# Eight expert rounds on one core: the two weight splits beside the last turned product are held back, and the output leaves in four transfers

## The reference

```python
def moe_swiglu(h, w_router, w_gate, w_up, w_down):
    ...
    logits = (xf @ w_router).astype(jnp.float32)
    top_logits, top_idx = lax.top_k(logits, TOP_K)      # TOP_K = 2
    gates = jax.nn.softmax(top_logits, axis=-1)
    ...                                                 # rows sorted by expert, in blocks of 128
    def expert_block(args):
        tok, e = args
        xb = xf[tok]
        hb = jax.nn.silu(xb @ w_gate[e]) * (xb @ w_up[e])
        return hb @ w_down[e]
    ...                                                 # weighted by the gates and added per token
```

## Time and profile before

| | us |
|---|---|
| median of 3 runs | 2028.63 |
| the three runs | 2028.44, 2028.63, 2031.82 |
| span of the profiled execution (first to last instruction) | 2030.7 |
| the only one of the three times that is longer than that span | 2031.82 |
| TensorE busy in the span | 1940.3 (96%) |
| VectorE busy | 1566.0 (77%) |
| ScalarE busy | 1241.0 (61%) |
| chain that ended last, TensorE's share | 84% |
| the eight rounds, from the first gate product to the last sum | about 985 |

### The profile page before, as it was taken

One profiled execution on the slowest core, in us unless ns is written; L12 is line 12 of the kernel. 1 busy time (PEld: TensorE's weight loads), 2 busy tenths in 40 slices (PEclk: granted clock), 3 DMA queues, 4 the chain that ended last, 5 costly groups with the idle time before them and its releaser, 6 DMA issues.

```text
span 2030.7 us, 26201 instructions
## 1 busy us (share of the span) xinstructions
PE 1940.3 (96%) x9320; PEld 1619.0 (80%) x9320; DVE 1566.0 (77%) x1881; ACT 1241.0 (61%) x1461; POOL 160.4 (8%) x228
## 2 busy tenths in 40 slices
PE   8989988899989899999999999999999999999998
PEld 6867877778778788888878878888888888888886
DVE  7765966867656654446878898989889898998987
ACT  5562145645654544344767767777777777777775
POOL 4113401313011000000000000000000000000000
PEclk9999999999989999999999999999999999999999
DMA  8422234324324255553459999899999989999994
GB/s 330 157 84 104 93 125 140 125 104 180 113 82 178 92 207 187 187 187 125 187 229 382 355 353 376 343 382 351 372 375 349 376 342 385 353 373 374 341 376 174
DMA packets 71802, 504.78 MB, mean 249 GB/s; under 512 B 8864, under 2 KB 8864, under 8 KB 11808
## 3 DMA queue, kind: packets, MB, share of 16 engines
q1 hardware_dynamic: 70432, 498.87, 64.8%
q0 software_dynamic: 1280, 4.72, 0.6%
HBM read 501.46 MB, written 2.10 MB: 248 GB/s over the span
## 4 chain that ended last, share of the span: by engine, by line
PE 84%; DVE 8%; ACT 5%; issue 2%; POOL 1%; DMA 0%; DVEq 0%; SPq 0%; ACTq 0%; POOLq 0%
PE psum L1022 24%; PE psum L1024 24%; PE psum L1023 24%; PE psum L1958 4%; DVE low L989 3%; ACT high L986 2%; PE psum L3486 1%; PE psum L1966 1%; ACT h L1694 1%; PE psum L3417 0%; PE psum L1974 0%; DVE small L1738 0%; PE psum L1566 0%; DMA const<-in_constants 0%; PE psum L1143 0%
## 5 line engine op out<-in xcount | busy, mean ns | idle before, releaser
L989 DVE TENSOR_TENSOR low<-raw,high 128x2048 fp32r<-128x2048 f32 x459 | 1044.9, 2281 | 265.5 <-ACT high L986 261.9
L986 ACT ACTIVATE high<-raw 128x2048 fp32r<-128x2048 f32 x459 | 876.9, 1912 | 371.3 <-PE psum L1024 352.6
L1022 PE MATMUL psum<-high,yT_high 128*128 128x512 f32 (+1 forms) x1672 | 664.6, 397 | 25.9 <-DVE yT_low L3695 6.5
L1024 PE MATMUL psum<-high,yT_low 128*128 128x512 f32 (+1 forms) x1672 | 653.3, 391 | 0.0
L1023 PE MATMUL psum<-low,yT_high 128*128 128x512 f32 (+1 forms) x1672 | 652.1, 390 | 0.0
L1022 PEld LDWEIGHTS psum<-high,yT_high 128*128 128x128 f32 x1672 | 315.5, 189 | 95.6 <-issue 14.2
L1024 PEld LDWEIGHTS psum<-high,yT_low 128*128 128x128 f32 x1672 | 315.3, 189 | 67.1
L1023 PEld LDWEIGHTS psum<-low,yT_high 128*128 128x128 f32 x1672 | 316.0, 189 | 61.0
L1022 PE MATMUL psum<-high,hT_high 128*128 128x512 f32 (+2 forms) x560 | 220.8, 394 | 1.6 <-DVE low L1006 0.9
L1024 PE MATMUL psum<-high,hT_low 128*128 128x512 f32 (+2 forms) x560 | 217.3, 388 | 0.0
L1023 PE MATMUL psum<-low,hT_high 128*128 128x512 f32 (+2 forms) x560 | 217.3, 388 | 0.0
(11 more groups left out here) (367 smaller groups left out, 1714.9 us busy)
## 6 DMA issues: line engine op xcount, KB each, us to landing
raw<-in_moe_weights SPq DMA_DIRECT2D x336, 1024.0 KB, 4.9
raw<-in_weights SPq DMA_DIRECT2D x132, 1024.0 KB, 4.9
raw<-in_weights SPq DMA_DIRECT2D x2, 896.0 KB, 4.7
raw<-in_weights SPq DMA_DIRECT2D x2, 768.0 KB, 8.1
x<-in_x SPq DMA_DIRECT2D x2, 512.0 KB, 3.9
raw<-in_weights SPq DMA_DIRECT2D x2, 512.0 KB, 3.6
rows<-h POOLq DMA_DIRECT2D x1, 1024.0 KB, 4.8
out_x<-x SPq DMA_DIRECT2D x1, 1024.0 KB, 5.5
```

Source lines behind the costliest of these rows:

```text
L986: eng.activation(high, raw, ACT.Copy).then_inc(k.high_ready, 1)
L989: eng.tensor_tensor(low, raw, high.bitcast(F32), ALU.subtract).then_inc(k.low_ready, 1)
L1022: pe.matmul(out, lhs.high, rhs.high, start=start, stop=False)
L1024: return pe.matmul(out, lhs.low, rhs.high, start=False, stop=stop)
```

## The change

Two things are changed. The steps that begin no split are now "down first 5" and turn 6, on ScalarE and on VectorE alike. And the store waits for each of the four scatter parts by itself and issues a transfer of 256 KB for it, before it waits for all four.

```diff
+HELD = (("down first", FF_STEPS - 2), ("turn", FF_STEPS - 1))
...
-def moe_wait_all(k, sp):
-
-    k.wait_released(sp, ("moe", "scatter", 3), (k.more + (N_EXPERTS - 1)) * 2)
+def moe_wait_scatter(k, sp, i):
+
+    k.wait_released(sp, ("moe", "scatter", i), (k.more + (N_EXPERTS - 1)) * 2)
...
-            if (kind, i) != ("turn", FF_STEPS - 1):
+            if (kind, i) not in HELD:
                 done = split_round(k, act, done, index, t)
...
-            if (kind, i) != ("turn", FF_STEPS - 1):
+            if (kind, i) not in HELD:
                 done = split_round(k, v, done, index, t)
...
+    rows = k.out[0].rearrange("(t p) d -> p t d", p=P)
     if layers[-1] == "moe":
-        moe_wait_all(k, sp)
-    else:
-        for name in out_names(layers[-1]):
-            k.wait_released(sp, name)
-    sp.dma_start(k.out[0].rearrange("(t p) d -> p t d", p=P), k.x[:, :, :]).then_inc(k.stored, 16)
+        for i in range(4):
+            moe_wait_scatter(k, sp, i)
+            half, tile = i // 2, i % 2
+            cols = slice(512 * half, 512 * (half + 1))
+            sp.dma_start(rows[:, tile, cols], k.x[:, tile, cols]).then_inc(k.stored, 16)
+        sp.wait_ge(k.stored, 64)
+        return
```

## The result

| | before | changed |
|---|---|---|
| median, us (5 runs each) | 2028.63 | 2037.83 |
| lowest and highest, us | 2025.77, 2031.82 | 2035.51, 2040.69 |
| ratio to before, 95% interval | | 1.0051 (1.0039 to 1.0062) |
| span of the profiled execution, us | 2030.7 | 2038.9 |

The change makes the kernel slower, by 9.2 us in the medians. The forecast was 2035.5, and 2037.83 lies in its range. In the experiments further down, one run of e3_hold_last (2195.32) and one of e4_short_gather (2203.34) were slow executions, with a mean granted clock of 0.85 and 0.84 instead of 0.99, and the ratios leave them out.

What follows compares the result with a forecast made beforehand. TensorE was taken as the bound, busy 84% of the span. Held splits cost 8.9 us and the store saves 2.0, so 6.9 more on the 2028.63 median gives 2035.5; range 2031.5 to 2039.5.

Steps and rivals of the forecast that it cites:

- Direction and mechanism: At each round's tail the turn's wait goes, but held splits delay down 6 and gate 0; 6.9 us slower in all.
- The common round: Rounds 1 to 6: gate 0 starts 1.2 us later, including 0.28 from down 6's later start.
- I give it no chance of its own: Rival that the clock falls behind a longer wait; dismissed because it was 1.00 around round 0's 2.2 us wait.
- Sum of the held splits: Loss over the rounds: 6 x 1.2 + 1.7 = 8.9 us, with round 7 losing nothing.
- upper bound of the forecast: Held splits' loss if VectorE's whole lag reached TensorE each time: 7 x 1.65 = 11.6 us.
- The wait behind round 0: TensorE's wait for granule 3, after VectorE's list of overfull experts: near 2.7 us instead of 2.2.
- The store: At the kernel's end, four 256 KB transfers instead of one of 1 MB: 2.0 us saved.
- a sign: At the kernel's end, the last of four stores should land 3 to 3.5 us after its issue.
- From span to time: Whole kernel: time about 1.1 us over span if the 2031.82 run was profiled; the difference was added to the median.
- ScalarE isn't the limit there: Before gate 0, ScalarE has the next round's high 0 at about 1895.1, ahead of VectorE's low from 1895.95.
- The loads: Loads into raw places freed some 3.4 and 3.1 us later at a round's tail: costed at nothing.
- The rival of the removed wait: Before down 6 the wait is simply removed: 7 x 0.95 + 2.0 = 8.7 us less, 2019.9; chance 0.05.

Runs made afterwards that it cites:

- e3_hold_last: The changed kernel, but only granule 41's split held until behind turn 6, granule 40 begun as before the change; 2025.53 us, ratio to before 0.9984.
- e4_short_gather: The changed kernel with six of eight pieces of the gathered tokens' low left out on VectorE in rounds 0 to 7; 2029.07 us, ratio to before 1.0009.
- e1: The changed kernel with the output leaving in one transfer as before, so only the two splits held; 2041.46 us, ratio to before 1.0052.
- e2: The changed kernel with the order of splits of before, so only the store in four transfers; 2025.35 us, ratio to before 0.9984.
- e5: The changed kernel with VectorE's list of overfull experts cut into five pieces beside gates 1 to 5 of round 0; 2032.29 us, ratio to before 1.0022.
- e8: The changed kernel with only granule 41 held and the next round's granule 0 split ahead of the gathered tokens; 2019.22 us, ratio to before 0.9955.
- e9: The changed kernel, both splits held, with the next round's granule 0 split ahead of the gathered tokens; 2033.31 us, ratio to before 1.0027.

## Why the prediction was right, and where it was short

- **Direction and mechanism were right.** Down 6 later by 0.23 in round 6 (1900.52 - 1898.30 = 2.22 behind the gather against 1.99; forecast 0.28), gate 0 later by 1.12 (forecast 1.2). The wait for the turn goes (6.5 us in seven waits, none after). Down 6 waits for low 40 instead, 1.18 where 1.24 was expected. Gate 0 waits behind VectorE's longer queue. e1 and e2 show that the hold is the whole loss.
- **The common round was 0.2 short** (1.39 against 1.2). Gate 0's distance from the gather grew by 1.12 in round 6 and by 8.88 - 7.54 = 1.34 in round 2 (1412.21 - 1403.33 after, 1407.95 - 1400.41 before). I took 0.08 between the end of a low and TensorE's start. In round 2 it is 0.24 (low 0 ends at 1411.97, the matmul starts at 1412.21), and the first matmul behind a wait holds its follower off by 0.34 instead of 0.23. The changed kernel has two waits a round where before had one, so it pays this once more.
- **"I give it no chance of its own" was wrong of the clock.** The step took round 0's 2.2 us wait with a clock of 1.00 as proof that a wait of this size is free. Behind a wait of 2.31 it was not: 1.6 us, which makes 3.24 of the expected 1.7 (VectorE's delay itself cost 1.63, as forecast). In e5, where the wait is gone, the clock stays at 1.00. What else it takes isn't known: the changed kernel had waits of 1.29 and 0.85 ahead of the 2.31, but e4 had 1.29 ahead of 2.33 and kept its clock, and e8 lost it with none ahead of 2.85.
- **Sum of the held splits:** forecast 8.9, trace 11.6; 1.6 of the gap of 2.7 is the clock, the rest the 0.2 in each of six rounds. That 11.6 is also the upper bound of the forecast (7 x 1.65) is a coincidence: VectorE's lag didn't reach TensorE in full each time.
- **The wait behind round 0** was to be near 2.7 and is 2.31. TensorE came to it 1.54 later than before (1.63 - 0.09), not 1.2, so that more of VectorE's 1.63 was already spent.
- **The store** was forecast at 2.0 and brought 1.8. The fixed 2.75 and 0.7 of data were nearly right: 3.45 against a longest landing of 3.7, just outside the 3 to 3.5 that were named as a sign, and 5.5 - 3.7 is the 1.8. The median landing of the four is 2.3, but the end counts the last one.
- **From span to time:** the profiled run was taken for the one at 2031.82, 1.1 over its span. In the changed kernel and in all runs of the experiments the time is 1.8 to 1.9 over the span, so it was none of the three. Nothing hangs on it, because the difference was added to the median.
- **"ScalarE isn't the limit there" held** for the changed kernel: high 0 ends at about 1903.8, 0.9 ahead of low 0's start at 1904.66. e4 shows it as the next limit.
- **The loads** were hidden, as costed: from 1150 us on, ScalarE's table of waits names no transfer in the changed kernel.
- **The rival of the removed wait** gave 0.95 a round as its price. e3 shows that even a turn and a low 40 in time would have brought only 0.3, since gate 0's own chain had only 0.6 to spare. Taken alone that rival was overpriced three times; with that chain moved ahead as well (e8) it was worth 1.18.

## What to carry to other kernels

A wait names the last thing that was late, not what it would bring to remove it: before an order is changed, measure how far ahead of its need each of the next two or three items is, since the smallest of these is all that can be won. When two engines work off a queue for a third, work held back for an urgent item is paid by everything behind it; hold back no more than the item needs (here one split of two), and then order the rest by when it is needed. A wait that is inherited from another cause (here a list of small instructions behind round 0) takes every delay in full, and is worth clearing away by itself.

## What was not expected of the hardware

- In six of the ten traces the wait behind round 0 is 2.3 us or more, and in five of these (changed, e1, e3, e8, e9, with waits of 2.31, 2.32, 2.33, 2.85 and 2.97) the granted clock falls for a few us behind it, in e3 and e8 from the first matmul on (0.80 and 0.79 long instead of 0.50); matmuls of 512 columns start 0.43 apart instead of 0.23. In e4, with 2.33, it stayed at 1.00, as in before and e2 with 2.22 and 2.21. What decides between e4 and the others stays open, and each kernel has one trace only.
- Runs of one kernel spread over 6 us (2024.89 to 2030.86 for the kernel before in the two groups), and the spread goes with the mean granted clock: its 20 runs with 0.990 or more have a median of 2026.0, its 27 runs below that 2029.9, and the two sets overlap by half a microsecond only. In the traces the part ahead of the rounds, identical in all, varies by 8 us, and its clock with it: from 550 to 600 us it is 0.97 in e3 and e4, which reach the first unplace at 1043.3 and 1044.6, and 0.90 to 0.93 in the other eight, which reach it between 1046.4 and 1051.2. The rounds of kernels with the same order of splits agree within 0.03 us in the mean (changed and e1, before and e2). Why the clock differs from run to run stays open.
